# Value rows weighted in their slots and summed by accumulating transposes, in a PEER decoder trunk on one core

## What is computed

```
q = (xt @ w_q).reshape(PEER_BLOCK, PEER_HEADS, 2, PEER_DK // 2)
s = jnp.einsum('thcd,hcnd->thcn', q, keys)
sv, si = lax.top_k(s, PEER_TOPK)
...
idx = jnp.take_along_axis(cand_i, top_p, axis=-1)
g = jax.nn.softmax(top_s, axis=-1)
a = jnp.einsum('td,thkd->thk', xt, u_tab[idx])
hk = (g * jax.nn.gelu(a, approximate=False)).astype(xt.dtype)
return jnp.einsum('thk,thkd->td', hk, v_tab[idx])
...
hp = layer_norm(DN_ALPHA * hp + peer_ffn(hp, ...), ln_g[i, 1], ln_b[i, 1])
```

## Time and profile before

| | us |
|---|---|
| median of 3 runs | 3224.0 (3223.45 to 3225.96) |
| span of the profiled execution | 3220.8 |
| PE busy | 2951.7 (92%) |
| DVE busy | 2302.1 (71%) |
| ACT busy | 1280.3 (40%) |
| POOL busy | 1245.2 (39%) |
| moved by DMA | 1236.60 MB, of which 1115.93 MB by the gathers |

### The profile page before, as it was taken

One profiled execution on the slowest core, in us unless ns is written; L12 is line 12 of the kernel. 1 busy time (PEld: TensorE's weight loads), 2 busy tenths in 40 slices (PEclk: granted clock), 3 DMA queues, 4 the chain that ended last, 5 costly groups with the idle time before them and its releaser, 6 DMA issues.

```text
span 3220.8 us, 33576 instructions
## 1 busy us (share of the span) xinstructions
PE 2951.7 (92%) x9366; PEld 1646.5 (51%) x9366; DVE 2302.1 (71%) x5862; ACT 1280.3 (40%) x3574; POOL 1245.2 (39%) x1100
## 2 busy tenths in 40 slices
PE   9998899989977989999898999999899787788998
PEld 7766555545533446554454455665455333334554
DVE  0663677777688878776767777767777888678655
ACT  0143333343334553333433563333434443344652
POOL 0100434544444434333434444434344454444441
PEclk9997999999999999999999999999999999999999
DMA  5523999999999999999999999999999999999996
GB/s 182 210 102 134 363 394 421 421 421 421 419 421 420 413 389 422 421 421 412 415 416 421 400 413 408 421 416 416 416 416 403 420 418 417 419 396 408 421 421 268
DMA packets 178123, 1236.60 MB, mean 384 GB/s; under 512 B 19918, under 2 KB 23758, under 8 KB 31632
## 3 DMA queue, kind: packets, MB, share of 16 engines
q0 software_dynamic: 156896, 1115.93, 84.3%
q1 hardware_dynamic: 20896, 117.47, 9.2%
q10 hardware_dynamic: 144, 1.05, 0.1%
HBM read 1227.91 MB, written 6.50 MB: 383 GB/s over the span
## 4 chain that ended last, share of the span: by engine, by line
PE 51%; DMA 28%; DVE 12%; ACT 3%; issue 2%; DVEq 2%; POOL 1%; ACTq 0%; SPq 0%; POOLq 0%
DMA arena<-in_uv,idx 28%; PE acc L1886 26%; PE bank L1923 9%; DVE arena L1654 7%; PE bank L1914 6%; PE bank L1709 4%; PE bank L1756 2%; PE acc L1895 1%; POOL arena L1032 1%; ACT L1186 1%; ACT diag L1208 1%; PE bank L1761 1%; PE acc L1780 1%; DVE arena L1662 1%; DVEq L1562 1%
## 5 line engine op out<-in xcount | busy, mean ns | idle before, releaser
L1886 PE MATMUL acc<-arena,diag 128*128 128x512 f32 x3912 | 1811.3, 612 | 186.9 <-ACT diag L1208 186.2
L1032 POOL DMA_INDIRECT arena<-in_uv,idx x1024 | 1195.3, 1167 | 1622.4 <-PE acc L1886 1329.9
L1654 DVE CUSTOM_DVE_ANT_0 arena<-arena,h 128x1024 f32<-128x1024 f32 x1024 | 1229.7, 1221 | 447.8 <-DMA arena<-in_uv,idx 442.9
L1886 PEld LDWEIGHTS acc<-arena,diag 128*128 128x128 f32 x3912 | 745.2, 195 | 1115.3 <-issue 798.5
L1192 ACT ACTIVATE act_w<-dots 128x2 f32<-128x2 f32 x520 | 105.8, 203 | 1476.8 <-DVE dots L1654 1476.5
L1923 PE MATMUL bank<-hT,panel 128*128 128x264 f32 (+2 forms) x1760 | 399.1, 380 | 2.2 <-DMA panel<-in_panels 1.4
L1923 PEld LDWEIGHTS bank<-hT,panel 128*128 128x128 f32 x1760 | 329.2, 191 | 87.9 <-issue 42.0
L1208 ACT ACTIVATE diag<-cst,act_w 128x128 f32<-128x128 f32 x980 | 342.0, 394 | 50.0 <-PE acc L1886 15.9
L1195 ACT ACTIVATE act_w<-act_w 128x1 f32<-128x1 f32 x1040 | 249.5, 286 | 44.4 <-issue 2.5
L1192 ACT ACT_TABLE_LOAD x130 | 166.8, 1283 | 2.0 <-issue 0.2
L1914 PE MATMUL bank<-panel,qT 128*128 128x256 f32 (+1 forms) x640 | 144.9, 380 | 0.0
(11 more groups left out here) (234 smaller groups left out, 2277.4 us busy)
## 6 DMA issues: line engine op xcount, KB each, us to landing
panel<-in_panels SPq DMA_DIRECT2D x94, 1024.0 KB, 9.1
arena<-in_uv,idx POOLq DMA_INDIRECT x1024, 19.9
arena<-in_cache_k POOLq DMA_DIRECT2D x16, 512.0 KB, 5.5
arena<-in_cache_v POOLq DMA_DIRECT2D x16, 512.0 KB, 4.8
arena<-in_panels SPq DMA_DIRECT2D x6, 1024.0 KB, 6.9
arena<-out_y_s POOLq DMA_DIRECT2D x8, 512.0 KB, 6.2
h<-in_h SPq DMA_DIRECT2D x1, 2048.0 KB
out_nv_p<-arena POOLq DMA_DIRECT2D x4, 512.0 KB, 2.9
```

The source lines that it names most:

```text
L1032: nc.gpsimd.indirect_dma_start(uv[:, slot_of(e), :], None, uv_dram[layer], bass.IndirectOffsetOnAxis(ids[:, r:r + 1], 0)).then_inc(gathere ...
L1654: V.tensor_tensor_reduce(uv[:, slot_of(e), 0:D], uv[:, slot_of(e), 0:D], x_rows, 1.0, 0.0, ALU.mult, ALU.add, dots[:, G % 2, r:r + 1]).the ...
L1886: m = mm(acc[:, half * 512:(half + 1) * 512], diag[:, r % DIAGS, :], uv[:, slot_of(e), D + half * 512:D + (half + 1) * 512], start=False, ...
```

## The change

ACT no longer makes a diagonal. It scales the v row in its slot (128x1024), for every expert but the last 8. PE no longer multiplies: it transposes each of the row's eight 128x128 chunks with the identity as the moving operand and lets the transposes accumulate in `acc`, which so holds the sums turned, [column, token]. Joined pairs, `add_joined`, `join_two` and the planner's load tables are gone.

```diff
-            def two_experts(G, q, mask):
+            def two_experts(G, q):
...
-                if (G, q) in plan.joined:
-
-                    r = 2 * q + 1
-                    row = uv[:, slot_of(G * GROUP + r), D:2 * D]
-                    nc.scalar.activation(row, row, ACT.Copy, scale=act_w[:, 2, half, r:r + 1]).then_inc(weighted, 2)
-                    return
                 for r in range(2 * q, 2 * q + 2):
-                    before = plan.turn_of_diag(G * GROUP + r)
-                    if before > 0:
-                        act.wait_ge(slot_done, before)
-                    nc.scalar.activation(diag[:, r % DIAGS, :], mask, ACT.Copy,
+                    e = G * GROUP + r
+                    if e < FIRST_BY_ROWS:
+                        row = uv[:, slot_of(e), D:2 * D]
+                        nc.scalar.activation(row, row, ACT.Copy, scale=act_w[:, 2, half, r:r + 1]).then_inc(weighted, 1)
+                        continue
+                    if e >= FIRST_BY_ROWS + DIAGS:
+                        act.wait_ge(slot_done, e - DIAGS + 1)
+                    nc.scalar.activation(diag[:, r % DIAGS, :], const("ident"), ACT.Copy,
                                          scale=act_w[:, 2, half, r:r + 1]).then_inc(weighted, 1)
+                if G * GROUP + 2 * q == FIRST_BY_ROWS:
+                    act.wait_ge(slot_done, FIRST_BY_ROWS)
+                    nc.scalar.activation(yb[:], acc[:], ACT.Copy).then_inc(turned_over, 1)
```

```diff
+            def add_two(G, q, sample):
+                for r in range(2 * q, 2 * q + 2):
+                    e = G * GROUP + r
+                    pe.wait_ge(weighted, e + 1)
+                    for c in range(C):
+                        row = uv[:, slot_of(e), D + c * P:D + (c + 1) * P]
+                        if sample:
+                            m = mm(acc[:, c * P:c * P + NS], row, const("group_of")[:, 0:NS], start=False, stop=True,
+                                   skip_group_check=True)
+                        else:
+                            m = mm(acc[:, c * P:(c + 1) * P], row, const("ident"), is_transpose=True, start=False, stop=True,
+                                   skip_group_check=True)
+                    m.then_inc(slot_done, 1)
```

Since the sums stand turned, three things are added. `start_tile` multiplies the row's chunks with alpha on the diagonal (8 matmuls of 128 columns in place of 2 of 512). At a tile's end ACT copies `acc` to `stage` (the tensor `lnb`) and not to `h`; two background pieces `back` in the next window's first lot turn it on PE and ACT copies the two banks to `h`:

```diff
+                elif x.kind == "back":
+                    pe.wait_ge(acc_free, place(x.layer, x.b) + 2)
+                    m = rows(x.b)
+                    for q in range(4):
+                        c = 4 * x.half + q
+                        last = nc.tensor.transpose(bank[0:m, x.n % BANKS, q * P:(q + 1) * P], stage[:, c * P:c * P + m],
+                                                   const("ident"))
+                    last.then_inc(bank_full, 1)
```

More of the change, by code:

```diff
@@ L159, in __init__ @@
         self.queries = {}
+        self.backs = {}
         for p in range(8):
@@ L201, in number, with back @@
                             self.release[x.panel] = ("bank", n)
+    def back(self, layer, b):
+        self.backs[place(layer, b)] = [self.product(Piece("back", layer=layer, b=b, half=half)) for half in range(2)]
+        return self.backs[place(layer, b)]
     def lead(self):
@@ L502, in build @@
         self.settle()
-        self.joined = {}
-        for kind, layer, b, lots in steps:
-            if kind == "window" and b < TB and layer + b > 0:
-                for t in joined_pairs(layer, b, lots):
-                    self.joined[first_group(layer, b) + t // 4, t % 4] = len(self.joined)
-        return steps
-    def turn_of_diag(self, e):
-        seen = e - DIAGS
-        while seen >= 0 and (seen // GROUP, seen % GROUP // 2) in self.joined:
-            seen -= DIAGS
-        return seen + 1
+        return steps
 def first_group(layer, b):
@@ L521, in first_group @@
     return layer * GROUPS + sum(HEADS * 2 if x < TB else 1 for x in before)
-def joined_pairs(layer, b, lots):
-    out, behind = [], 0
-    parts = [part for _, _, _, _, part in window_pairs(layer, b, lots)]
-    for t in range(1, len(parts) - LAST_STEPS):
-        part = parts[t]
-        behind += sum(map(tensor_load, part)) - PAIR_ROOM - 5 * sum(x.product and x.panel is not None and x.kind != "turn" for x in part)
-        behind = max(behind, 0)
-        near = sum(map(vector_load, parts[t])) + sum(map(vector_load, parts[t - 1]))
-        if behind > JOIN_GAIN and near <= JOIN_ROOM and (not out or out[-1] < t - 1):
-            out.append(t)
-            behind -= JOIN_GAIN
-    return out
 def window_pairs(layer, b, lots):
@@ L1238, in _ @@
                 act.wait_ge(slot_done, (G + 1) * GROUP)
-                nc.scalar.activation(h[0:rows(b), b, :], acc[0:rows(b), :], ACT.Copy).then_inc(acc_free, 1)
+                done = place(layer, b)
+                if done == 0:
+                    act.wait_ge(ln_done, BLOCKS)
+                else:
+                    act.wait_ge(bank_full, plan.backs[done - 1][1].n + 1)
+                m = rows(b)
+                nc.scalar.activation(stage[:].rearrange("p (c t) -> p c t", c=C)[:, :, 0:m],
+                                     acc[:].rearrange("p (c t) -> p c t", c=C)[:, :, 0:m], ACT.Copy).then_inc(acc_free, 1)
         @block.vector
@@ L1862, in start_tile, with turn_over @@
                 pe.wait_ge(acc_free, count)
[L1863 to L1865 removed]
+                for c in range(C):
+                    mm(acc[:, c * P:(c + 1) * P], src[:, c * P:(c + 1) * P], const("alpha_eye"),
+                       start=(c % 4 == 0), stop=True, skip_group_check=True)
+            def turn_over():
+                pe.wait_ge(turned_over, 1)
+                for c in range(C):
+                    mm(acc[:, c * P:(c + 1) * P], yb[:, c * P:(c + 1) * P], const("ident"), is_transpose=True,
+                       start=(c % 4 == 0), stop=True, skip_group_check=True)
             def add_last(G, q):
```

77 lines of the change are left out of this document (26 added, 51 removed).

## The result

The changed kernel takes 3233.7 us (median of 8 runs, 3230.3 to 3237.3), the one before 3223.7 in the same rounds (8 runs, 3222.0 to 3226.0). The ratio is 1.0032, with a 95% interval of 1.0022 to 1.0042: some 10 us slower. The prediction had 3219.5, a gain of 4.7 us in the profile, and had given a chance of 0.25 to a kernel slower by more than can be told. The profiled execution has a span of 3230.3 us against 3220.8.

The account below looks back on a forecast made before the run. DMA transfers were taken to bound the kernel, with 22 us idle. Regained 9.5 less 4.8 for the exponential gave -4.7 from 3220.8: 3216.1 profiled, plus 3.2, stated as 3219.5 us; own range 3214 to 3226, whole range 3206 to 3246.

Parts of the forecast that it names:

- The bound: Expert stage: DMA transfers bind, not PE at 92% busy; only 22 us of missing DMA share could be won.
- the sample's experts: Sample tiles, 16 experts: 1.8 to 7.4 us of PE each, low end taken; the high end adds 88 us, mostly hidden.
- 9.5 us regained: Idle DMA time won back: 3.0 in the first window, 3.5 from 1960 to 2500, 3.0 in three other stretches.
- The exponential: End of each route: DVE waits 1.5 us longer for ACT's exponential, costing 4.8 us in all.
- the ring: The 11 gather slots, 27 us of transfers mostly in flight, were to cover a 4.9 us debt from 2500 to 2740.
- `back` at nothing: Turning the sums back, 9 times: eight transposes of 0.9 to 1.7 us in all, counted as no cost.
- Sizes: Per-engine work: transposes 0.11 us apart, an expert 0.88 us of PE, PE about 970 us less, ACT about 2050 us.
- C: Stretches with sigmoids, 415 us: ACT late for one pair in six, +14 less 5, giving 3233; chance 0.10.
- B: Every route: DVE becomes the bound through the exponential, +26 less 5, giving 3245; chance 0.10.
- A: Expert stage: slots free sooner, three quarters of the 22 us idle time comes back, giving 3210; chance 0.30.
- D: PE's clock: transposes do not raise it, so it stays low wherever sums prevail, +510, giving 3730; chance 0.06.
- E: PE's sums: an accumulating transpose runs as two passes, 1.75 us an expert as before, giving 3228; chance 0.04.

Follow-up runs that it names:

- e8_wide: The changed kernel with the sample's products 128 columns wide in place of 8; ratio 1.0002 to the kernel before the change.
- e14_half_adds: e8_wide with PE adding only the first four of each row's eight chunks; ratio 0.9993 to the kernel before the change.
- e10_plain: The changed kernel with the prompt's transposes replaced by ordinary products with the identity moving; ratio 1.0170 to the kernel before the change.

## Why the prediction was wrong

**The bound: right.** The page's PE share misled, and DMA binds. PE was busy for 474 us less, and the kernel gained nothing by it.

**The step that failed: the sample's experts, costed at nothing.** The prediction put a record between 0.11 and 0.46 us and took the low end, 1.8 us an expert, beside a ring that hides it. It measured 0.20 us a record in the mean, 3.2 us an expert. The row it leaned on, the turns' step of 0.11 us, was at the full clock, and narrow records do take 0.10 there; but from 1780.8 on the granted clock was 0.50, and they took 0.21, the step that the earlier trace rows gave for the low clock. With it the tile would have been 8 x 3.4 = 27 us of PE work in a window that lasted 20, and the cover argued away: in the last pairs of the tile nothing lies beside them, ACT waits for them and the next tile for ACT. "All but some 10 us a tile" hidden was about the right size for the stall itself (9.4 and 17.4 us longer), but it was priced at the high end only and left out of the sum. Some 5 us of the second tile's 17.4 are its late start behind `back`. At the end of the kernel the narrow form measured 6 to 10 us.

**The step that failed beside it: 9.5 us regained.** The shares of 1180 to 1260 and 1960 to 2500 rose by more than the forecast had counted, 0.05 x 80 = 4 and 0.01 x 540 = 5 us where it took a third and two thirds. But the first window, counted with 3.0, gave nothing: its share is 0.94 as before, although POOL's waits there shrank (13.18 and 7.55 in the earlier trace rows; changed kernel, start us, us, wait in brackets):

```profile
400.22 0.93 POOL L989 DMA_INDIRECT arena<-in_uv,idx  x1 [11.24 <-PE acc L1867]
...
411.23 0.94 POOL L989 DMA_INDIRECT arena<-in_uv,idx  x1 [6.35 <-PE acc L1867]
```

These gathers are issued later than before (400.22 for 398.21), with a shorter wait ahead: a wait that shrinks is no gain when what precedes it came later. And the gain elsewhere was lost again at 700, 1050 and in the lean stretches. Where the width is mended both sum to nothing (1.0000, 1.0002), and half the work on both engines left out yields some 5 us where 22 us of idle share seemed to be for the taking. Reading the missing share as available time was the error: a stretch's shortfall says when the queue was short, not that PE made it so.

**The exponential: the wait right, its cost mis-sized.** Forecast near 175 us, measured 189.2. Priced +2.8 at 1180 to 1260, where the share rose to 1.01 instead, and +1 at 2500 to 2740, where it fell by 0.02 x 240 = 5 us and half the wait removed brought it back to 1.01. The debt of 4.9 us there was not bridged by the ring. Taking half of it away let the gathers catch up by 2740, but the tile ended at the same time, so how much of it reaches the end is open; with the early copies to `h` it is 3 to 4 us.

**`back` at nothing: wrong in place, small in sum.** Its own two steps hold little; what the prediction did not look at are the banks, which it holds for two steps of ACT, so that the products behind it wait 2 to 4 us, and POOL waits 12 to 14 us for the next gather where it waited 7.5 before. When that alone went, the end did not move measurably.

**Sizes.** Transposes: 0.11 us steps at the full clock, right (eight in 1.04 us of the start at 704.11). ACT 2034.9 against about 2050. PE busy for 77% and not 60 to 75, and its work 474 us less and not 970: an expert took 1.23 us of PE and not 0.88, part of it the mean clock of 0.86. The text expected a low clock in lean stretches and yet summed at the full one. Its last sum is off by a little too: 3216.1 and 3.2 make 3219.3, not 3219.5.

**Rivals.** C's 3233 is the measured time by chance. Of its two stretches 2940 to 3175 kept a share of 1.01 with ACT busy for 196 of 235 us, and 1780 to 1960 came back to the share of before in e8_wide, with ACT as busy as in the changed kernel (147.10 us):

```profile
1780.00:1960.00 180.00, 148.74 (x903) 121.36 (x902) 127.17 (x293) 149.49 (x240) 80.80 (x68) 0.90 0.99 407
```

B is right about one place, 2500 to 2740, not about the size. A did not come: the time did not fall. D is wrong: at 2500 to 2740, PE's work the same but for the transposes of the sums, twice as many of them raise the granted clock from 0.52 to 0.74 (e14_half_adds here, e8_wide's row stands above):

```profile
2500.00:2740.00 240.00, 109.06 (x432) 72.61 (x432) 201.59 (x583) 165.82 (x289) 114.22 (x92) 0.52 0.99 401
```

Transposes do count here. The Trainium skill says otherwise (TensorE: Matmul & The Clock Gate, Part 4: PE-mode transpose: the high clock "doesn't engage" for transposes); by it, the time would have been rival D's 3730, and the measurement decides. E did not occur, as each transpose is one record; its two passes were tried in e10_plain: some 55 us (1.0170), where its 3228 had 4; with ACT's rows in it PE is busy for 94% of the span.

## What to carry to other kernels

Cost each small product at the clock that will be granted where it stands: a run of 8-column f32 products kept PE full while its clock fell to the low level, and sixteen times the columns finished sooner. Look at the shortest tile first when a form of work is changed everywhere; here nothing lay beside its last products to cover them. And before pricing idle transfer time as gain, leave half the work out once: that bound (some 5 us here) would have told that little was to be had.

## What the runs showed of the hardware

- 64 products of 8 columns (128 records): 25.5 us, granted clock 0.54 in the mean while PE was busy for 99.8% of the stretch; 0.10 us a record at 1.00, 0.21 at 0.50. The same with 128 columns: 14.8 us at 1.00.
- Halving the number of transposes in a stretch that had little else lowered the granted clock from 0.74 to 0.52, and PE's busy time only from 140 to 109 us.
- An f32 product of 128 columns is two records of some 0.11 to 0.12 us each (e8_wide, e10_plain), a transpose of the same operands one of 0.11 at the full clock.
- Two runs of a kernel may differ by 7 us in 3230 with nothing changed (3230.3 to 3237.3), and the same kernel before has medians of 3222.6 to 3227.1 us on different chips; only ratios in the same rounds tell 0.1 to 0.3%.
